# Two blocks of layers in fp32 on one core: order of the head's loads and squares, form of the last norm, and which engine makes the gate weights' remainders

## Chip, cores, metric

The kernel runs on one NeuronCore of a Trainium2 chip. The metric is the device time of one launch in microseconds; the median of several runs is compared. Engines are called TensorE (PE), VectorE (DVE), ScalarE (ACT), GpSimd (POOL) and SyncE (SP, which here issues DMAs).

## What is computed

256 tokens of width 1024 go through a first block (three mixers whose gated outputs are summed, and a feed-forward with a squared ReLU) and a second one (a convolution and pooling mixer, then a gated linear recurrence), all in fp32. What the change touches:

```python
def first_block(x, ...):
    h = rms_norm(x, norm1_g[l])          # the head
    u = h @ w_in[l]
...
def odd_mixer(h, w_in, conv_w, conv_b, w_rg, b_rg, w_ig, b_ig, lam, w_out):
    p = jnp.einsum("btd,dn->btn", h, w_in)
    xr, gate = jnp.split(p, [W_LRU], axis=-1)
    xc = causal_depthwise_conv(xr, conv_w, conv_b)
...
    _, hs = lax.associative_scan(_lin_combine, (a, bterm), axis=1)
    y = hs.astype(h.dtype) * jax.nn.silu(gate)
    return jnp.einsum("btn,nd->btd", y, w_out)
...
    return rmsnorm(h, final_norm)        # the last norm, 8 chunks of 128 features
```

## The kernel before

Activations lie transposed, 128 features by 256 tokens to a chunk, in a large SBUF tensor `arena`. A projection ("job") makes one chunk of outputs out of blocks of 128x128 weights. Eight blocks are a unit of 512 KB; SyncE fetches units 0 to 285 in order into a ring of five (`ring`, `RING`), unit `u` when the job that used unit `u - 5` is done.

Each fp32 product is made of three matmuls of fp32r parts: high weights by high data, high by low, low by high (L1750 to L1752). For that ScalarE copies a unit to its high part (`wsplit`, L887, `ring_hi`, three slots), and then GpSimd or VectorE subtracts to get the remainder (`remainder`, L553, written to `ring_lo`). Which of the two does a unit is said by `on_gpsimd`, in part by the unit's turn `hi_turn`, which counts from 1. Activations are split in the same way: high part on ScalarE (L908 with a gain, L910 without), remainder on VectorE (L1111) or GpSimd (L561).

`schedule()` writes one list of steps, and each engine goes through the whole list in order and does its own part of each step, waiting on semaphores. So an instruction that waits holds up all that stands behind it on its engine. A unit's `wsplit` stands `AHEAD` = 2 units before its job; that of the first two stood before the step `("nsq", 0, 4)`.

The head: `spin` is idle work for TensorE, `fills` are zero fills on VectorE, `split`/`lo` of `h0u` make x times its gain in two parts (not yet divided by the norm; the first eight jobs are scaled afterwards by `scale`, L1118), `nsq` squares a chunk on VectorE (L1078), `nsum` sums it on TensorE (L1504), `norm` is the root on ScalarE (L767) and the reciprocal on VectorE (L1094). `halves` are seven small scalings of parameters (L1081 to L1090). Then follow the token projections `tok` (L1515), the key norms `qsq`/`qap` (L1542, L1203), the compression inputs `cmp_in` (L1190) and matmuls `cmp_mm` (L1533), among the first `dq` jobs.

Near the end are twelve `xr` jobs (units 250 to 261), twelve `gate` jobs (262 to 273) and eight `odd_out` jobs of twelve blocks (274 to 285). In the xr loop VectorE does the convolution `oconv` (L1324 to L1330), the norm's `hf` (L1102) and `lw` (L1431, L1432); ScalarE the four functions of `rgi` (L949 to L955). In the gate loop VectorE does, for each job, `scan` (product L1443 of two SBUF chunks, scan L1444), `scanout` of two jobs before (L1437) and `gact` (L1455); ScalarE a tanh (L1009) and the split of `ly`, three jobs behind; GpSimd the remainder of that split (L561). Nine roots (`uroot`, L930) stand before gate job 0 and three behind job 5, each with a change of the function table. `rinv` (SBUF) and `rin` (PSUM) hold the reciprocal norm.

The last norm: after `odd_out` VectorE writes the reciprocal to PSUM and makes eight outputs with `hf` (L1102: chunk times gain times `rin`), stored two at a time.

## Time and profile before

| | us |
|---|---|
| median of 3 runs (1119.0 to 1123.94) | 1119.44 |
| the profiled execution | 1117.76 |
| its span, first to last instruction | 1116.0 |
| TensorE busy in the span | 1061.0 |
| VectorE busy | 725.9 |
| GpSimd busy | 603.5 |
| ScalarE busy | 591.6 |
| mean granted TensorE clock, of full speed | 0.981 |

Times in the trace are us from the span's start. A busy time includes time in which an instruction has started and is held by something outside its semaphores. "Idle before" is the time an engine stood still ahead of an instruction, with the instruction that ended it. TensorE's matmuls overlap, so their own lengths add up to more than their pace.

### The profile page before, as it was taken

To read this page: it belongs to the slowest core of one execution; us is meant where nothing else is said; L and a number is where in the kernel's file an instruction comes from. 1 tells how busy PE (TensorE), PEld (TensorE's weight loads), DVE (VectorE), ACT (ScalarE), POOL (GpSimd) and SP (SyncE) were. 2 spreads that over 40 slices of the span, in tenths; PEclk is the share of its full clock that TensorE was granted. 3 is DMA by queue.
4 is the path that set the end of the run, shared out by engine and by line. 5 is a ranking of instruction groups with operands and counts; after the bars stand their busy time and mean duration, and the time that the engine had idled before them with its cause. 6 is when DMAs were issued, how large, how long until landed. Compare 5 with 4: busy or idle time off the path is not lost. (4 is left out here: it accounts for less than half of the span.)

```text
span 1116.0 us, 21390 instructions
## 1 busy us (share of the span) xinstructions
PE 1061.0 (95%) x8189; PEld 996.0 (89%) x8189; DVE 725.9 (65%) x1494; ACT 591.6 (53%) x1178; POOL 603.5 (54%) x457
## 2 busy tenths in 40 slices
PE   8999999999999999989999999999998788999996
PEld 8799888888889998979999999999988787999986
DVE  7749587666653325784575553334999878678964
ACT  5335566766665467753445554335333436468741
POOL 3536444454445469544533444338677665467951
PEclk9989999999999999999999999999999989899999
DMA  8324332333233443235555555555444434544442
GB/s 302 99 89 139 126 115 95 114 115 114 97 113 127 139 133 100 91 99 173 183 161 181 187 183 177 182 178 170 157 164 154 130 113 132 176 146 146 156 136 74
DMA packets 43157, 158.08 MB, mean 142 GB/s; under 512 B 4912, under 2 KB 4912, under 8 KB 42672
## 3 DMA queue, kind: packets, MB, share of 16 engines
q1 hardware_dynamic: 42912, 156.69, 42.5%
q8 instruction: 65, 1.06, 0.4%
q14 instruction: 36, 0.29, 0.1%
q10 hardware_dynamic: 144, 0.03, 0.0%
HBM read 155.65 MB, written 1.05 MB: 140 GB/s over the span
## 5 line engine op out<-in xcount | busy, mean ns | idle before, releaser
L1750 PE MATMUL p_proj<-arena_r,ring_hi 128*128 128x256 f32 x2208 | 660.0, 299 | 19.9 <-POOL ring_lo L553 8.2
L1751 PE MATMUL p_proj<-arena_r,ring_hi 128*128 128x256 f32 x2208 | 627.7, 284 | 0.0
L1752 PE MATMUL p_proj<-arena_r,ring_lo 128*128 128x256 f32 x2208 | 627.6, 284 | 0.0
L553 POOL TENSOR_TENSOR ring_lo<-ring,ring_hi 128x1024 fp32r<-128x1024 f32 x182 | 437.0, 2402 | 308.0 <-ACT ring_hi L887 307.0
L1750 PEld LDWEIGHTS p_proj<-arena_r,ring_hi 128*128 128x128 f32 x2208 | 426.1, 193 | 39.3 <-issue 23.1
L1751 PEld LDWEIGHTS p_proj<-arena_r,ring_hi 128*128 128x128 f32 x2208 | 426.6, 193 | 8.1 <-issue 6.0
L1752 PEld LDWEIGHTS p_proj<-arena_r,ring_lo 128*128 128x128 f32 x2208 | 426.1, 193 | 0.0
L887 ACT ACTIVATE ring_hi<-ring 128x1024 fp32r<-128x1024 f32 x276 | 290.5, 1053 | 116.1 <-PE p_proj L1752 114.6
L553 DVE TENSOR_TENSOR ring_lo<-ring,ring_hi 128x1024 fp32r<-128x1024 f32 x94 | 118.4, 1260 | 70.7 <-ACT ring_hi L887 69.3
L661 POOL TENSOR_TENSOR sbuf_s<-sbuf_s,srow 128x256 f32<-128x256 f32 (+1 forms) x48 | 42.8, 892 | 83.5 <-DVE srow L1312 58.9
L910 ACT ACTIVATE arena_r<-arena 128x256 fp32r<-128x256 f32 x108 | 42.7, 409 | 44.8 <-DVE arena L1477 22.3
L561 POOL TENSOR_TENSOR arena_r<-arena,arena_r 128x256 fp32r<-128x256 f32 x64 | 51.5, 814 | 21.5 <-ACT arena_r L910 21.5
L908 ACT ACTIVATE arena_r<-arena,par 128x256 fp32r<-128x256 f32 x48 | 23.8, 505 | 63.4 <-DVE arena L1484 47.5
L1484 DVE TENSOR_TENSOR arena<-arena,p_proj 128x256 f32<-128x256 f32 x40 | 16.8, 421 | 62.3 <-PE p_proj L1752 61.6
L1300 DVE CUSTOM_DVE_ANT_0 sbuf_s<-p_score,caus,nrq 128x128 f32<-128x128 f32 (+1 forms) x64 | 24.2, 415 | 41.3 <-PE p_score L1595 39.3
L1399 DVE SCALAR_TENSOR_TENSOR p_score<-arena,par,p_score 128x256 f32<-128x256 f32 x116 | 46.9, 482 | 1.4
L1009 ACT ACTIVATE th<-p_proj 128x256 f32<-128x256 f32 x44 | 16.8, 383 | 54.4 <-PE p_proj L1752 54.4
L833 ACT ACTIVATE sbuf_s<-sbuf_s,srow 128x128 f32<-128x128 f32 (+1 forms) x96 | 42.6, 450 | 3.1 <-DVE srow L1300 3.1
L1737 PE MATMUL p_proj<-arena,ring 128*128 128x256 f32 x160 | 38.0, 390 | 5.7 <-issue 5.7
L1737 PEld LDWEIGHTS p_proj<-arena,ring 128*128 128x128 f32 x160 | 30.2, 195 | 10.4 <-issue 6.5
L1125 DVE SCALAR_TENSOR_TENSOR arena<-p_proj,rinv 128x256 f32<-128x256 f32 x32 | 13.6, 424 | 37.2 <-PE p_proj L1752 37.2
L561 DVE TENSOR_TENSOR arena_r<-arena,arena_r 128x256 fp32r<-128x256 f32 x44 | 27.1, 616 | 15.2 <-ACT arena_r L910 13.8
(272 smaller groups left out, 1218.4 us busy)
## 6 DMA issues: line engine op xcount, KB each, us to landing
ring<-w_stream SPq DMA_DIRECT2D x286, 512.0 KB, 3.3
arena<-w_tok SPq DMA_DIRECT2D x1, 1632.0 KB, 13.0
arena<-w_rgi SPq DMA_DIRECT2D x1, 1536.0 KB, 6.6
arena<-x_t SPq DMA_DIRECT2D x4, 256.0 KB, 4.8
arena<-w_cmp SPq DMA_DIRECT2D x1, 1024.0 KB, 16.3
out_t<-arena SPq DMA_DIRECT2D x4, 256.0 KB, 2.4
par<-cols SPq DMA_DIRECT2D x1, 323.0 KB, 3.3
row<-rows ACTq DMA_DIRECT2D x1, 32.0 KB, 3.5
```

The costliest lines, as they stand in the source:

```text
L553: return eng.tensor_tensor(ring_lo[:, u % RING, :, :].rearrange("p k n -> p (k n)"), ring[:, u % RING, :, :].rearrange("p k n -> p (k n)") ...
L561: return eng.tensor_tensor(lo(c), src(c), hi(c).bitcast(F32), ALU.subtract)
L661: pool.tensor_tensor(p, p, r.unsqueeze(2).to_broadcast([P, 2, kl]), ALU.mult)\
L833: ins = act.activation(p, p, ACT.Exp, bias=srow[:, i % 4, 2 + h:3 + h], scale=-1.0, accum_out=srow[:, i % 4, 4 + h:5 + h])
L887: act.activation(ring_hi[:, hi_slot[u], :, :].rearrange("p k n -> p (k n)"), ring[:, u % RING, :, :].rearrange("p k n -> p (k n)"), ACT.Copy)\
L910: ins = act.activation(hi(c), src(c), ACT.Copy)
L1300: ins = dve.tensor_tensor_reduce(out=x[:, h, :], in0=ps[:, h, :], in1=mask[:, t, 0:kl], scale=nrq[:, n:n + 1], scalar=-MARK, op0=ALU.add, ...
L1399: ins = dve.scalar_tensor_tensor(out=A(AC + cc) if tap == CONV_K - 1 else acc, in0=ub[:, cc, tap:tap + S], scalar=col("even_cw", CONV_K * ...
L1737: mm = pe.matmul(slot(s)[:, 0:S], ring[:, u % RING, b % 8, :], rhs[c], start=(c == 0), stop=(c == n - 1))
L1750: pe.matmul(slot(s)[:, 0:S], w_hi, hi, start=(c == 0), stop=False)
L1751: pe.matmul(slot(s)[:, 0:S], w_hi, lo, start=False, stop=False)
L1752: mm = pe.matmul(slot(s)[:, 0:S], w_lo, hi, start=False, stop=(c == n - 1))
```

## The change

Five things. In the head, SyncE fetches weight unit 0 before x and units 1 on behind it; the steps `wsplit` of units 0 and 1 get places of their own (`("units", 0)` before the splits of x, `("units", 1)` behind them), all eight squares stand behind both, all eight sums behind the first job, and the idle work of TensorE is 20 in one place instead of 12 and 10. `halves` moves from behind the eighth scaling to the seventh job (`n == 6`). The remainders of the first eight units, which went to VectorE at odd turns and to GpSimd at even ones, are swapped. The remainders of the gate units, all on GpSimd, go by turn; unit 262 has turn 253, so units 262, 264, ... 272 are VectorE's and 263, ... 273 GpSimd's. In the last norm ScalarE multiplies each chunk by its gain (`xg`, behind its root), and VectorE multiplies two chunks at once by the reciprocal norm (`hfin`); the stores wait for those. The last norm's reciprocal is written to PSUM as before.

```diff
--- before.py
+++ after.py
@@ -68,7 +68,7 @@
 ADDED_BY = {"h1": "w_out", "h2u": "ff2", "h3u": "even_ya"}
 
 
-HF_ROUND = {0: 0, 2: 1, 3: 2, 4: 3}
+HF_ROUND = {0: 0, 2: 1, 3: 2}
 
 
 PLAIN = {"b_val", "pool"}
@@ -106,26 +106,25 @@
         if tag:
             out.append(("lo", tag, 7))
 
-    out += [("spin", 12), ("fills", 0)]
+    out += [("spin", 20), ("fills", 0), ("units", 0)]
     for c in range(8):
-        if c < 4:
-            out += [("nsq", 0, c), ("split", "h0u", c), ("nsum", 0, c), ("lo", "h0u", c)]
-        else:
-            out += [("split", "h0u", c), ("lo", "h0u", c)]
-    out += [("spin", 10)] + [("nsq", 0, c) for c in range(4, 8)]
+        out += [("split", "h0u", c), ("lo", "h0u", c)]
+    out += [("units", 1)] + [("nsq", 0, c) for c in range(8)]
     for n, job in enumerate(HEAD):
         out.append(job)
         if n == 0:
-            out += [("nsum", 0, c) for c in range(4, 8)] + [("norm", 0)]
+            out += [("nsum", 0, c) for c in range(8)] + [("norm", 0)]
         else:
             out.append(("scale", HEAD[n - 1]))
         if 1 <= n <= 4:
             out += [("hf", 0, 2 * n - 2), ("hf", 0, 2 * n - 1)]
         if n == 4:
             out += [("fills", 1)]
+        if n == 6:
+            out.append(("halves",))
         if n >= 4:
             out += [("split", "h0", 2 * n - 8), ("split", "h0", 2 * n - 7)]
-    out += [("scale", HEAD[7]), ("halves",)]
+    out += [("scale", HEAD[7])]
     out += [("ksq", 0), ("ksq", 1), ("cmp_in", 0), ("tok", 0), ("qsq", 0), ("cmp_in", 1), ("qap", 0), ("ksq", 2),
             ("tok", 1), ("qsq", 1), ("cmp_in", 2), ("cmp_in", 3), ("qap", 1)]
     keys = {0: [("cmp_mm",)], 1: [("qsq", 2)], 2: [("qap", 2), ("ksq", 3)], 3: [("qsq", 3)], 4: [("softplus",)],
@@ -283,7 +282,7 @@
             out.append(("split", "ly", j - 3))
     out += [("scanout", 10), ("scanout", 11)] + [("split", "ly", c) for c in range(9, 12)]
     squared(4, jobs["odd_out"])
-    out += [("nsum", 4, 7), ("norm", 4)] + [("hf", 4, c) for c in range(8)] + [("store",)]
+    out += [("nsum", 4, 7), ("norm", 4)] + [("xg", c) for c in range(8)] + [("hfin", c) for c in range(0, 8, 2)]
 
     at, splits = 0, {}
     order = [s for s in out if s[0] == "job"]
@@ -293,7 +292,7 @@
     units = len(starts) // 8
     for u in range(units):
         if starts[8 * u][1] not in PLAIN:
-            splits.setdefault(("nsq", 0, 4) if u < AHEAD else starts[8 * (u - AHEAD)], []).append(("wsplit", u))
+            splits.setdefault(("units", u) if u < AHEAD else starts[8 * (u - AHEAD)], []).append(("wsplit", u))
     final = []
     for s in out:
         final += splits.get(s, []) + [s]
@@ -536,8 +535,10 @@
                 unit_of.setdefault(b // 8, s[1])
 
         def on_gpsimd(u):
-            if unit_of[u] in ("br_dsa", "dq", "nq", "val_glu", "b_gate", "a_gate", "even_yb", "xr", "gate"):
+            if unit_of[u] in ("br_dsa", "dq", "nq", "val_glu", "b_gate", "a_gate", "even_yb", "xr"):
                 return True
+            if unit_of[u] in ("iq", "ik", "dk", "kc", "vc", "ks", "kw"):
+                return hi_turn[u] % 2 == 1
             if unit_of[u] in ("xbc",):
                 return hi_turn[u] % 3 > 0
             return hi_turn[u] % 2 == 0
@@ -583,9 +584,10 @@
         @block.sync
         def _(sp_eng):
             sp_eng.dma_start(par[:, :], cols).then_inc(sem("par_in"), 16)
-            for c in range(0, 8, 2):
-                sp_eng.dma_start(arena[:, XT + c:XT + c + 2, :], x_t[:, c:c + 2, :]).then_inc(sem(f"x_in{c}"), 16)
             for u in range(n_units):
+                if u == 1:
+                    for c in range(0, 8, 2):
+                        sp_eng.dma_start(arena[:, XT + c:XT + c + 2, :], x_t[:, c:c + 2, :]).then_inc(sem(f"x_in{c}"), 16)
                 if u == RING:
                     sp_eng.dma_start(wtok, w_tok).then_inc(sem("wtok_in"), 16)
                     sp_eng.dma_start(wcmp, w_cmp).then_inc(sem("wcmp_in"), 16)
@@ -597,7 +599,7 @@
                 sp_eng.dma_start(ring[:, u % RING, :, :].rearrange("p k n -> p (k n)"),
                                  w_stream[u]).then_inc(w_in[u % RING], 16)
             for c in range(0, 8, 2):
-                sp_eng.wait_ge(sem("hf_ready"), 8 * HF_ROUND[4] + c + 2)
+                sp_eng.wait_ge(sem("out_ready"), c // 2 + 1)
                 sp_eng.dma_start(out[:, c:c + 2, :], arena[:, HF + c:HF + c + 2, :]).then_inc(sem("stored"), 16)
             sp_eng.wait_ge(sem("stored"), 64)
 
@@ -942,6 +944,11 @@
                     if j >= 4:
                         act.wait_ge(sem("lo_ff"), j - 3)
                     act.activation(A(FFS + j % 4), A(FFR + j % 4), ACT.Square).then_inc(sem("ffs_ready"), 1); note(sem("ffs_ready"))
+                elif k == "xg":
+                    c = s[1]
+                    was_read(act, ("job", "odd_out", c), "D")
+                    act.activation(A(HH + c), A(XT + c), ACT.Identity, scale=col("final_g", c))\
+                        .then_inc(sem("xg_ready"), 1); note(sem("xg_ready"))
                 elif k == "rgi":
                     h = s[1]
                     ps = take(s)
@@ -1068,7 +1075,7 @@
             ths = [0]
             for s in steps:
                 k = s[0]
-                if k not in ("nsq", "lo", "hf"):
+                if k not in ("nsq", "lo", "hf", "hfin"):
                     settle()
                 if k == "nsq":
                     _, q, c = s
@@ -1094,14 +1101,19 @@
                     link(dve.reciprocal(rin if s[1] == 4 else rinv[:, :], root[:, 0, :]))
                 elif k == "hf":
                     _, q, c = s
-                    if c == 0 and q < 4:
+                    if c == 0:
                         link(dve.tensor_scalar(rin, rinv[:, :], 1.0, None, ALU.mult))
                     if q == 0:
                         dve.wait_ge(sem("par_in"), 16)
-                    g = {0: "norm1", 2: "even_g", 3: "odd_g", 4: "final_g"}[q]
+                    g = {0: "norm1", 2: "even_g", 3: "odd_g"}[q]
                     dve.scalar_tensor_tensor(out=A((HF0 if q == 0 else HF) + c), in0=A(XT + c), scalar=col(g, c),
                                              in1=rin, op0=ALU.mult, op1=ALU.mult)\
                         .then_inc(sem("hf_ready"), 1); note(sem("hf_ready"))
+                elif k == "hfin":
+                    c = s[1]
+                    dve.wait_ge(sem("xg_ready"), c + 2)
+                    dve.tensor_tensor(A(HF + c, 2), A(HH + c, 2), rin.unsqueeze(1).to_broadcast([P, 2, S]), ALU.mult)\
+                        .then_inc(sem("out_ready"), 1); note(sem("out_ready"))
                 elif k == "lo":
                     _, tag, c = s
                     src, hi, lo, _, _ = parts[tag]
```

## Rows read from the trace of the kernel before

**Rows 1.** The page, its first part: busy us, share of the span, instructions.
```profile
PE 1061.0 (95%) x8189; PEld 996.0 (89%) x8189; DVE 725.9 (65%) x1494; ACT 591.6 (53%) x1178; POOL 603.5 (54%) x457
```

**Rows 2.** Stretches: busy us (count) of PE, PEld, DVE, ACT, POOL; PEclk; DMA share; GB/s.
```profile
20.00:38.20 18.20, 18.20 (x153) 18.20 (x152) 11.05 (x23) 11.82 (x24) 11.62 (x8) 1.00 0.60 201
38.20:56.46 18.26, 14.93 (x61) 9.41 (x60) 17.41 (x31) 3.88 (x8) 7.74 (x7) 1.00 0.16 55
56.46:63.40 6.94, 6.94 (x65) 6.88 (x65) 3.56 (x5) 0.00 (x0) 0.00 (x0) 0.50 0.04 15
...
63.60:66.60 3.00, 3.00 (x15) 3.00 (x16) 0.00 (x0) 1.40 (x4) 1.50 (x1) 0.50 0.00 0
...
1041.00:1064.00 23.00, 22.12 (x173) 20.86 (x171) 21.97 (x30) 16.48 (x28) 21.87 (x15) 1.00 0.49 166
```

**Rows 3.** Time line of the head: start us, length us, engine, line, operation.
```profile
8.41 2.57 DVE L1111 SCALAR_TENSOR_TENSOR arena_r<-arena,par,arena_r 128x256 fp32r<-128x256 f32 x5
...
9.15 0.91 ACT L908 ACTIVATE arena_r<-arena,par 128x256 fp32r<-128x256 f32 x2 [0.97 <-DMA arena<-x_t]
...
10.66 1.06 ACT L887 ACTIVATE ring_hi<-ring 128x1024 fp32r<-128x1024 f32 x1 [0.60 <-DMA ring<-w_stream]
...
13.06 2.40 POOL L553 TENSOR_TENSOR ring_lo<-ring,ring_hi 128x1024 fp32r<-128x1024 f32 x1 [6.91 <-ACT ring_hi L887]
...
13.08 3.67 DVE L1078 TENSOR_TENSOR arena<-arena 128x256 f32<-128x256 f32 x4
...
13.20 1.06 ACT L887 ACTIVATE ring_hi<-ring 128x1024 fp32r<-128x1024 f32 x1 [0.22 <-DMA ring<-w_stream]
...
17.67 0.47 PE L1750 MATMUL p_proj<-arena_r,ring_hi 128*128 128x256 f32 x1
```

**Rows 4.** Time line behind the head; in brackets the idle time before and its releaser.
```profile
38.28 0.43 DVE L1118 TENSOR_TENSOR p_proj<-p_proj,rinv 128x256 f32<-128x256 f32 x1 [2.45 <-PE p_proj L1752]
...
44.56 0.70 PE L1542 MATMUL p_pv<-th,mean_h 128*128 128x256 f32 x2 [0.91 <-DVE th L1198]
...
56.46 6.99 PE L1533 MATMUL p_score<-arena 128*64 128x30 f32 x64 [2.42 <-DVE arena L1190]
```

**Rows 5.** L1443 alone (DVE busy, PEclk, DMA, GB/s); L1443, L561: ns min/median/max.
```profile
1020.00:1070.00 50.00, 15.32 (x12) 1.00 0.48 158
...
L1443 DVE TENSOR_TENSOR p_turn<-arena x4: 432/1566/2482, 1028.0 to 1059.5; 128x256 f32<-128x256 f32 x4
...
L561 POOL TENSOR_TENSOR arena_r<-arena,arena_r x64: 713/740/1777, 31.0 to 1070.7; 128x256 fp32r<-128x256 f32 x64
```

**Rows 6.** Time lines of ScalarE, GpSimd and VectorE from the xr projections on.
```profile
1018.39 0.43 DVE L1324 TENSOR_TENSOR p_proj<-p_proj,rinv 128x256 f32<-128x256 f32 x1
...
1019.53 1.05 ACT L887 ACTIVATE ring_hi<-ring 128x1024 fp32r<-128x1024 f32 x1
...
1031.71 0.43 DVE L1431 SCALAR_TENSOR_TENSOR p_score<-p_score,arena 128x256 f32<-128x256 f32 x1 [2.52 <-ACT arena L955]
...
1045.40 2.40 POOL L553 TENSOR_TENSOR ring_lo<-ring,ring_hi 128x1024 fp32r<-128x1024 f32 x1
...
1048.64 2.40 POOL L553 TENSOR_TENSOR ring_lo<-ring,ring_hi 128x1024 fp32r<-128x1024 f32 x1
...
1062.74 1.23 DVE L553 TENSOR_TENSOR ring_lo<-ring,ring_hi 128x1024 fp32r<-128x1024 f32 x1
...
1069.06 0.88 DVE L1437 SCALAR_TENSOR_TENSOR arena<-p_pv,arena 128x256 f32<-128x256 f32 x2
```

**Rows 7.** Time line of the last norm, and the group of L1345.
```profile
1108.16 1.76 DVE L1094 RECIPROCAL p_mean<-root 128x256 f32<-128x256 f32 x1 [1.37 <-ACT root L767]
...
1109.96 3.22 DVE L1102 SCALAR_TENSOR_TENSOR arena<-arena,par,p_mean 128x256 f32<-128x256 f32 x8
...
L1345 DVE TENSOR_TENSOR arena<-p_turn,sp 128x512 f32<-128x512 f32 x8 | 5.5, 691 | 4.1 <-PE p_turn L1634 3.9
```

## Prediction

> **What bounds the kernel now.** I read the page first, then the busy time in stretches, then the time lines of the four engines side by side where the diff touches them, at both ends and in the gate projections. TensorE is busy 95% of the span [rows 1], so the static list of matmuls sets the time, and a change can only pay in the places where TensorE waits or runs at its lower clock. The stretches show which places near the diff are like that [rows 2]: from 38.20 to 56.46 TensorE has 14.93 of 18.26 us busy while VectorE has 17.41; from 56.46 to 63.40 it is busy but at half the clock; from 1041 to 1064 VectorE has 21.97 of 23.00 us and GpSimd 21.87, with TensorE at 22.12. Everywhere else near the edits the four engines have room.
>
> One mechanism decides all parts. A subtraction of a whole weight unit costs 2.40 us on GpSimd and 1.23 us on VectorE [rows 3, 6], but a VectorE instruction with both inputs in SBUF stands still while GpSimd works, and the other way round. The squares at 13.08 are four instructions of some 0.43 us and take 3.67 us, because GpSimd holds from 13.06 to 15.46 [rows 3]. In the gates the product L1443 takes 1566 ns in the median of its form and 432 ns undisturbed [rows 5]. The instructions with an operand in PSUM (L1437, L1455) show no such stretch. At 1062.74 VectorE's subtraction starts and GpSimd's part, ready at the same time, waits for it.
>
> **The head: first weights ahead of x.** Before, the last of x has landed at 9.15 and unit 0 at 10.66, as the starts of ScalarE's copies show [rows 3]. The bytes up to the last of x and unit 0 are the same, so I let x's last piece land at about 10.4 and unit 0 at about 5.5. GpSimd (unit 0 now has its turn) subtracts from 6.65 to 9.05; this holds back VectorE's eight remainders of x, which have both inputs in SBUF. They cost 2.57/5 = 0.51 us each [rows 3], so they run from 9.05 to 13.1, and the first projection, chunk by chunk behind them, ends at about 13.5 instead of 16.1. The rest gives that back. VectorE does unit 1 next (13.1 to 14.35). ScalarE's copy of unit 2 ends at 14.26 as before [rows 3], GpSimd waits with unit 2 and takes the port until 16.75, and only then come the squares, now eight instead of four: 16.75 + 8 x 0.43 = 20.2. All eight sums stand in TensorE's list ahead of the second projection, which so starts at about 20.55 instead of 17.67: **+2.9**. In this gap TensorE has one sum to do in about 3.5 us. The clock fell at 56.46 after an idle time of 2.42 us [rows 2, 4], so I expect it to fall here too. A projection matmul takes 3.00/15 = 0.20 us then against 18.20/153 = 0.12 us [rows 2]; some 3.4 us at the low level cost about **+1.5** (0 if it does not fall, +3.0 if it stays down twice as long).
>
> The seven projections after that are one unbroken row (17.67 to 38.2) and only shift. Behind them VectorE is late: after 38.28 it does the halvings, with TensorE idle 0.91 at 44.56 and 2.42 at 56.46 [rows 4]. The halvings move ahead of that, into VectorE's idle time (2.45 us of it stand before 38.28, and more behind the earlier projections). Then VectorE is no longer late and both stalls go: **-3.3** (between -2.0, if another subtraction lands on L1190, and -3.3). Without the 2.42 us of idle time the compression matmuls (L1533, 64 of them in 6.99 us at the low clock) start at the high one. No row shows them there: at best 3.5 us are saved and 1.5 more on the projection behind them, at least nothing. Their 30 columns are few, and they kept the clock down for 7 us, so I take half of 5.0: **-2.5**. Head: +2.9 + 1.5 - 3.3 - 2.5 = **-1.4**, between -5.4 (2.9 - 3.3 - 5.0) and +3.9 (2.9 + 3.0 - 2.0). The second batch of VectorE's zero fills and the longer spin cost nothing: both lie in time in which their engine has no data yet.
>
> **The gates.** Before, all twelve remainders are GpSimd's. One round is 1048.64 - 1045.40 = 3.24 us on GpSimd, against 24 x 0.12 = 2.88 on TensorE, and VectorE, whose own share is 3.24 - 1.14 = 2.10, waits 1.57 - 0.43 = 1.14 us for the port in its product [rows 5, 6]. VectorE also ends the stage: its last two scan outputs end at 1069.94 [rows 6], and TensorE waits for what follows from them. So I count VectorE's chain. It gets six subtractions of 1.26 with their gaps: +7.6. Unit 262 comes first, where the convolution of 1018.39 stands now, but ScalarE's copy of it runs from 1019.53 to 1020.58 [rows 6]: +2.3 of waiting. Unit 264 must wait until the copies behind the nine roots are done, and takes up the 2.52 us that VectorE idles before 1031.71: -2.5. The port waits of before, 15.32 - 12 x 0.43 = 10.2 us in twelve products [rows 5], go: -10.2. New ones come. In a pair of rounds VectorE has 2 x 2.10 + 1.26 = 5.46 us to do with its two products 1.6 to 1.7 us from the next port user on either side, and GpSimd's 2.40 us fit in no such hole. I walked the four queues from 1018.39 to the end with these durations, letting whoever waits take the port first. It gave ten port waits of 0.2 to 0.9 us, 4.8 to 6.2 us together by how the durations are rounded. With 5.3 the last scan output ends at about 1072.4, **+2.5**: 7.6 + 2.3 - 2.5 - 10.2 + 5.3. In this walk two subtractions (units 268 and 272) meet GpSimd's part within 0.05 us. If GpSimd is first, its own subtraction then slips in behind, and VectorE's next product waits 2.4 us: +1.75 each. At 1062.74 VectorE was first by 0.04 us. I add half a case: **+3.4**, between -2.5 (TensorE's pace in all seven saturated rounds, 7 x 0.36) and +6.0 (both).
>
> The Trainium skill, SBUF — State Buffer, "Who interferes with whom", calls this a lock which whoever starts first holds for its whole instruction, with the other fully blocked. By that rule alone two rounds hold the port 2 x (2.40 + 0.74 + 0.35) = 7.0 us before and 2.40 + 1.23 + 2 x 1.09 = 5.8 us after, so an estimate from port time alone would be a gain of 3 to 4 us; the trace's two rounds of 6.48 us are shorter than the rule's 7.0, so a part of the small instructions overlaps. What speaks against that gain is VectorE's order, which the rule leaves out. The same skill, Perfetto Trace Analysis, "Optimizing Scalar/DVE Operations", warns that moving work between these two engines might not help, since they share a read port.
>
> **The last norm.** Before, the reciprocal ends at 1109.92 and eight products take 3.22 us to 1113.18 [rows 7]. After, four products of two chunks: the nearest row is L1345, 691 ns for 128x512 with one operand in PSUM; 4 x 0.69 + 3 x 0.03 = 2.85. ScalarE's eight gains stand behind its root (which ends 0.1 us before 1108.16) in its queue; at 0.45 us each [rows 3] the last ends at 1111.65, and the fourth product, due at 1112.05, is not held. The store follows the last product as before: **-0.4** (0 to -0.8).
>
> **Sum.** -1.4 + 3.4 - 0.4 = +1.6 us. The profiled execution took 1117.76 us for its span of 1116.0, and the median of the runs is 1119.44, so it is 1.7 below it; I add the sum to the median: **1121.0 us**.
>
> **Rivals.**
> - *The gates pay.* TensorE gets its 2.88 us rounds, since GpSimd has 2.40 + 2 x 0.74 = 3.9 us [rows 5] in 5.76, and VectorE's waits vanish: -2.5 for the saturated rounds, and up to -1.2 in the first four. With the best head (-5.4) this is -8 to -9, **1111**. For it: GpSimd goes from one subtraction to the next without a gap. Against: VectorE has no gap there either, and its own 5.46 us leave 0.3 us in 5.76.
> - *The remainders are trapped* (the other side: slower). Each VectorE subtraction waits for GpSimd's part and then lets GpSimd's 2.40 us in ahead of the next product. It decides when GpSimd is first at units 268 and 272: gates +6.0; with a clock that stays down for two stretches in the head and no gain at the compression, +3.9 there: **1129** at worst, 1124 with the middle head.
> - *The head only loses.* The start is late by 4.4 to 5.9 and only the stalls of 3.3 come back: +1.1 to +2.6 instead of -1.4, total **1123.5 to 1125**. It decides if the compression runs at 1.2 GHz as before.
> - *Nothing is seen.* Both ends move inside the waits and the gates keep 3.24 us: **1119**.
>
> **How the numbers follow.** The forecast (parts nearly cancel, 1118 to 1123) has 0.50; the gates pay 0.14; trapped 0.12; the head only loses 0.14; nothing is seen 0.10. The bound of 0.5%, about what a measurement of this kernel tells from no change, is 5.6 us. Only the far ends of the first two rivals pass it, and an unknown clock fall adds to both: faster 0.12, same 0.76, slower 0.12. The range takes the forecast, the head's loss and the near halves of the two others: 1114.5 to 1126.
>
> **What would show it.** Right: the second projection starts at 20 to 22 us; VectorE's squares stand in one block after GpSimd's unit 2; TensorE has no idle time at L1542 and L1533; six L553 on VectorE between 1018 and 1064, one with over 2 us of waiting for ScalarE; the last L1437 later than 1069.9 relative to the tenth xr projection; four hfin products of 0.69 us. Wrong: the squares end by 18 us (then the head gains 2 to 3 us more); gate projections 2.88 us apart with VectorE idle between products; a clock that stays low for some 10 us in either place, which I could not bound from the rows.

## The result, and the profile after

| | before | after |
|---|---|---|
| median of 20 runs each, us | 1118.26 | 1122.61 |
| lowest and highest | 1115.78 to 1123.94 | 1119.9 to 1126.01 |
| the profiled execution, its span | 1117.76, 1116.0 | 1121.83, 1120.1 |
| mean granted TensorE clock | 0.981 | 0.977 |

The ratio is 1.0039 with a 95% interval of 1.003 to 1.0049: the change costs about 4.4 us, between 3.4 and 5.5. That lies inside the 5.6 us that I had called no change. The forecast was 1121.0, with a sum of +1.6 us. Line numbers move by 1 to 12: L553 is L554 now, L887 L889, L1078 L1085, the halvings (L1081 to L1090) L1088 to L1097, L1094 L1101, L1190 L1202, L1437 L1449, L1443 L1455, L1504 L1516, L1533 L1545, L1750 L1762; the last products are L1115.

The busy time in stretches after the change (us, busy time and instructions of five engines, granted clock, DMA share, GB/s); the third to fifth answer to [rows 2]:

```profile
16.60:19.00 2.40, 2.39 (x9) 2.05 (x10) 2.30 (x7) 0.00 (x0) 0.00 (x0) 0.80 0.99 418
19.00:21.70 2.70, 2.70 (x10) 2.14 (x8) 0.00 (x0) 0.00 (x0) 0.00 (x0) 0.55 0.82 331
42.60:60.40 17.80, 14.86 (x62) 9.65 (x61) 17.10 (x29) 4.69 (x11) 7.98 (x7) 1.00 0.18 61
60.40:65.80 5.40, 5.39 (x65) 5.34 (x65) 3.57 (x5) 0.00 (x0) 0.00 (x0) 0.69 0.01 3
1043.50:1066.50 23.00, 22.60 (x177) 21.38 (x176) 21.84 (x35) 16.15 (x28) 17.22 (x12) 1.00 0.54 176
1073.00:1080.00 7.00, 6.87 (x32) 6.67 (x33) 4.32 (x5) 3.55 (x5) 4.04 (x4) 0.53 0.11 28
```

The gap that the halvings were to close is still open (TensorE 14.86 of 17.80 us), the compression has a mean clock of 0.69, and the gates run a little fuller (22.60 of 23.00 us against 22.12). The time lines of the head, to be set beside [rows 3] and [rows 4]; the last line is the same place in the time line of TensorE:

```profile
13.98 4.92 DVE L1085 TENSOR_TENSOR arena<-arena 128x256 f32<-128x256 f32 x8
13.94 2.34 POOL L554 TENSOR_TENSOR ring_lo<-ring,ring_hi 128x1024 fp32r<-128x1024 f32 x1 [5.18 <-ACT ring_hi L889]
16.61 5.41 PE L1516 MATMUL p_mean<-arena,mean_d 128*128 128x256 f32 x16 [3.26 <-DVE arena L1085]
21.67 0.47 PE L1762 MATMUL p_proj<-arena_r,ring_hi 128*128 128x256 f32 x1
60.41 5.36 PE L1545 MATMUL p_score<-arena 128*64 128x30 f32 x64 [2.95 <-DVE arena L1202]
```

GpSimd's unit 2 starts 0.04 us ahead of the squares and the first sum can begin only at 16.61, behind it. From there it is not the squares that count, as I had thought: they end at 18.90, while the eight sums (two records each) take 5.41 us, part of them at the low clock, and the second projection starts at 21.67, 4.00 us later than before. The row of projections behind it is not unbroken either: TensorE waits 0.37 us at 36.78 for a remainder from GpSimd.

What VectorE then does ahead of the token projections:

```profile
37.75 0.90 DVE L1130 TENSOR_TENSOR p_proj<-p_proj,rinv 128x256 f32<-128x256 f32 x2
38.68 0.37 DVE L1088 TENSOR_SCALAR half<-par 128x16 f32<-128x16 f32 x1
...
40.52 2.31 DVE L1092 TENSOR_SCALAR par<-par 128x24 f32<-128x24 f32 x1
42.86 0.64 DVE L1094 TENSOR_TENSOR half<-par 128x8 f32<-128x8 f32 x1
...
44.21 2.28 DVE L1097 TENSOR_SCALAR half<-par 128x3 f32<-128x3 f32 x1
46.52 0.90 DVE L1130 TENSOR_TENSOR p_proj<-p_proj,rinv 128x256 f32<-128x256 f32 x2
```

The seven halvings run from 38.68 to 46.49 without a pause and hold up the last two scalings until 46.52. The last projection of the head is over at 42.6, so VectorE is late much as before (4.8 us, against 5.8 from 38.28 to 44.08). Then the gates, and TensorE's waits in and behind them:

```profile
1023.20 1.23 DVE L554 TENSOR_TENSOR ring_lo<-ring,ring_hi 128x1024 fp32r<-128x1024 f32 x1 [2.33 <-ACT ring_hi L889]
1027.08 0.38 PE L1762 MATMUL p_proj<-arena_r,ring_hi 128*128 128x256 f32 x1 [1.60 <-DVE arena L1342]
1035.38 0.38 PE L1762 MATMUL p_proj<-arena_r,ring_hi 128*128 128x256 f32 x1 [0.56 <-DVE arena L1342]
1053.28 1.23 DVE L554 TENSOR_TENSOR ring_lo<-ring,ring_hi 128x1024 fp32r<-128x1024 f32 x1
1054.54 0.85 DVE L1455 TENSOR_TENSOR p_score<-arena 128x256 f32<-128x256 f32 x1
1059.66 1.22 DVE L554 TENSOR_TENSOR ring_lo<-ring,ring_hi 128x1024 fp32r<-128x1024 f32 x1
1072.31 0.88 DVE L1449 SCALAR_TENSOR_TENSOR arena<-p_pv,arena 128x256 f32<-128x256 f32 x2
1114.37 2.48 DVE L1115 TENSOR_TENSOR arena<-arena,p_mean 128x512 f32<-128x512 f32 x4
```

VectorE waits 2.33 us for the copy of unit 262, as forecast, and the convolutions behind it are late, so TensorE waits 1.60 and 0.56 us for their results (L1342); before, it waited 0.42 us in this stretch. A pair of rounds is 1059.66 - 1053.28 = 6.38 us against 6.48. The four last products take 2.48 us instead of 3.22.

**Where the time went.** Every weight unit has one copy on ScalarE (L889 after, L887 before). How much later it starts than the copy of the same unit in the first trace of before gives a course through the execution. Columns are times of the trace before; "gates" is the difference between 1019.5 and 1062.6.

| later than before by, us | 36.2 | 69.7 | 496 | 834 | 1019.5 | 1062.6 | 1096 | end of span |
|---|---|---|---|---|---|---|---|---|
| after | 4.77 | 2.40 | 2.39 | 0.65 | 2.51 | 3.24 | 4.41 | 4.06 |
| E1 head alone | 5.11 | 2.75 | 2.80 | 1.05 | 2.52 | 2.54 | 2.52 | 2.52 |
| E2 gates alone | -0.40 | -0.21 | -0.17 | -0.88 | 3.74 | 4.47 | 4.45 | 4.47 |
| E3 norm alone | -0.31 | -0.11 | -0.08 | -0.80 | 1.10 | 1.12 | 1.16 | 0.80 |
| E4 halvings at the seventh job | -0.67 | -2.48 | -2.45 | -2.44 | 0.42 | 0.44 | 0.50 | 0.51 |
| E5 sums late | 2.63 | 1.76 | 1.81 | 0.08 | 1.69 | 2.42 | 3.57 | 3.21 |
| E6 idle work in the gap | 3.37 | 2.52 | 2.56 | 1.91 | 3.23 | 3.97 | 5.12 | 4.76 |
| E7 halvings at the start | 5.62 | 1.63 | 1.66 | -0.06 | 1.85 | 2.58 | 3.77 | 3.40 |
| E8 two units back | -0.16 | 0.05 | 0.08 | 0.11 | 0.26 | 2.77 | 3.19 | 3.22 |
| E9 halvings early, norm | 1.14 | -2.50 | -4.52 | -3.04 | -1.83 | -1.78 | -1.86 | -2.22 |
| E10 other turn | -0.42 | -1.74 | -1.71 | -2.35 | 1.61 | 3.16 | 2.22 | 2.24 |
| E11 before, again | -0.42 | -0.39 | -2.37 | -2.36 | -0.69 | -0.60 | -0.63 | -0.62 |

The last row is the scale for all others: the same kernel, profiled twice, moves against itself by up to 2 us in places that no edit touches. The difference over the gates alone repeats much better: they cost 0.73 or 0.74 us in all five kernels that have the changed turns (after, E2, E5, E6, E7), and at most 0.09 where they are untouched. The column 69.7 does not repeat so well: with the head of before it stands between -0.39 and 0.05 in E2, E3, E8 and E11, and at -1.74 in E10, whose clock stayed low for a shorter time at the compression.

### The profile page after: what moved, and what is told of

It is laid out like the page before. It is cut to its first block and busy times, and to the rows that moved or that the text cites. A ratio compares the mean times of both kernels' runs of the same rounds, so it can differ in the third digit from the quotient of the medians.

```text
span 1120.1 us, 21393 instructions
## 1 busy us (share of the span) xinstructions
PE 1063.5 (95%) x8185; PEld 998.3 (89%) x8185; DVE 733.2 (65%) x1496; ACT 594.6 (53%) x1186; POOL 593.8 (53%) x451
## 3 DMA queue, kind: packets, MB, share of 16 engines
HBM read 155.65 MB, written 1.05 MB: 140 GB/s over the span
## 5 line engine op out<-in xcount | busy, mean ns | idle before, releaser
L1762 PE MATMUL p_proj<-arena_r,ring_hi 128*128 128x256 f32 x2208 | 662.2, 300 | 18.7 <-POOL ring_lo L554 7.6
L554 POOL TENSOR_TENSOR ring_lo<-ring,ring_hi 128x1024 fp32r<-128x1024 f32 x176 | 424.4, 2413 | 318.6 <-ACT ring_hi L889 317.8
L1762 PEld LDWEIGHTS p_proj<-arena_r,ring_hi 128*128 128x128 f32 x2208 | 427.6, 194 | 38.1 <-issue 19.8
L889 ACT ACTIVATE ring_hi<-ring 128x1024 fp32r<-128x1024 f32 x276 | 290.5, 1053 | 117.2 <-PE p_proj L1764 114.1
L554 DVE TENSOR_TENSOR ring_lo<-ring,ring_hi 128x1024 fp32r<-128x1024 f32 x100 | 124.5, 1245 | 71.6 <-ACT ring_hi L889 70.0
L562 POOL TENSOR_TENSOR arena_r<-arena,arena_r 128x256 fp32r<-128x256 f32 x64 | 54.1, 855 | 24.9 <-ACT arena_r L912 24.8
L912 ACT ACTIVATE arena_r<-arena 128x256 fp32r<-128x256 f32 x108 | 42.6, 408 | 45.5 <-DVE arena L1489 22.5
L835 ACT ACTIVATE sbuf_s<-sbuf_s,srow 128x128 f32<-128x128 f32 (+1 forms) x96 | 42.6, 450 | 3.1 <-DVE srow L1312 3.1
```

What stands on the lines that cost most here:

```text
L554: return eng.tensor_tensor(ring_lo[:, u % RING, :, :].rearrange("p k n -> p (k n)"), ring[:, u % RING, :, :].rearrange("p k n -> p (k n)") ...
L562: return eng.tensor_tensor(lo(c), src(c), hi(c).bitcast(F32), ALU.subtract)
L835: ins = act.activation(p, p, ACT.Exp, bias=srow[:, i % 4, 2 + h:3 + h], scale=-1.0, accum_out=srow[:, i % 4, 4 + h:5 + h])
L889: act.activation(ring_hi[:, hi_slot[u], :, :].rearrange("p k n -> p (k n)"), ring[:, u % RING, :, :].rearrange("p k n -> p (k n)"), ACT.Copy)\
L912: ins = act.activation(hi(c), src(c), ACT.Copy)
L1762: pe.matmul(slot(s)[:, 0:S], w_hi, hi, start=(c == 0), stop=False)
```

## The experiments

Times are medians; ratios are against runs of before on the same chip, with 95% intervals. They are not the quotients of the medians, from which they differ by up to 0.001 (E4). E1 to E4 and E8 to E10 are built on the kernel before, E5 to E7 on the changed one.

**E1, the head part alone** (every hunk of the diff on the head, loads and turns of the first eight units; nothing else).

> The kernel before with the whole head part alone (loads, squares and sums behind job 0, halves at the seventh job, swapped turns). Theory A (the loss of the change lies mostly in the head): the trace of the changed kernel shows TensorE 2.4 us later behind the compression matmuls and the offset is 2.5 us before the gates, so this kernel is +2.5 us against before (ratio 1.0022), between +2 and +3.5. Theory B (the head is neutral and the loss comes from the gates and clock falls far behind it): within 1 us of before.

1122.48 against 1118.69 us, ratio 1.0042 (1.0025 to 1.0059). The trace is 2.75 us late behind the compression and 2.5 at the end; the time says 2.8 to 6.6 us. The head loses, and theory B falls. No run takes the head's own parts (loads, swapped turns, squares) one by one; E5 to E7 move the sums, the idle work and the halvings.

**E2, the gate turns alone.**

```diff
-            if unit_of[u] in (..., "even_yb", "xr", "gate"):
+            if unit_of[u] in (..., "even_yb", "xr"):
                 return True
```

> The kernel before with the gate remainders by turn, nothing else. Theory A (VectorE's chain is a little longer, as the changed kernel's last scan output 0.74 us later relative to its offset, and a second stretch at the low clock behind it): +0.7 us from VectorE and up to +1.2 from the clock, so +0.7 to +2.0 us. Theory B (the longer low clock behind the gates in the changed kernel has nothing to do with the turns): +0.7 us and a low stretch of one piece as before. Rival (gates pay): -2.5 or better.

1120.63 us, ratio 1.0014 (1.0000 to 1.0029). In the trace the stage costs 0.73 us; the low clock behind it is one short piece as before, so the longer one after the change (0.53 over 7 us, above) is not the turns' alone. The other 2.8 us of this trace come between 972 and 997 us, where nothing was changed: its clock falls at 986, and E10, the only other trace with that fall, loses the same there. The gates do not pay.

**E3, the last norm alone** (the hunks with `xg`, `hfin`, `out_ready`).

> The kernel before with the last norm's new form alone. Theory A: four products of 0.60 to 0.62 us instead of eight of 0.40, -0.7 us. Theory B: the gains on ScalarE delay the products or the stores land later, so nothing of it reaches the end: 0 +- 0.3 us.

1117.9 us, ratio 0.9998 (0.9986 to 1.0009). The time cannot tell; the trace can: from 1096 us to the end it gains 0.36 us (1.16 to 0.80), and after, E5, E6, E7 and E9, which have this norm too, gain 0.35 to 0.38. Theory A has the products right (-0.74) and forgets that half of it is lost behind them: from the last product to the end of the span it takes 3.25 us after the change, against 2.86 before.

**E4, only the place of the halvings.**

```diff
+        if n == 6:
+            out.append(("halves",))
...
-    out += [("scale", HEAD[7]), ("halves",)]
+    out += [("scale", HEAD[7])]
```

> The kernel before with the step halves moved to the seventh job, nothing else. My prediction's step: the halvings fall into VectorE's idle time before 38.28, both TensorE stalls of 0.91 and 2.42 us go and the compression matmuls start at the high clock: -3.3 to -6 us. Rival (what the changed kernel's trace hints at: the halvings run in port waits beside GpSimd's subtractions and push VectorE's scalings behind them): one stall goes, the other stays, -2 to 0 us.

1118.29 us, ratio 1.0006 (0.9992 to 1.0019). VectorE's time line, and TensorE's at the compression:

```profile
33.25 0.89 DVE L1083 TENSOR_SCALAR half<-par 128x16 f32<-128x16 f32 x1
...
35.60 2.29 DVE L1087 TENSOR_SCALAR par<-par 128x24 f32<-128x24 f32 x1
...
39.27 2.28 DVE L1092 TENSOR_SCALAR half<-par 128x3 f32<-128x3 f32 x1
41.59 0.90 DVE L1120 TENSOR_TENSOR p_proj<-p_proj,rinv 128x256 f32<-128x256 f32 x2
55.51 5.73 PE L1535 MATMUL p_score<-arena 128*64 128x30 f32 x64 [2.85 <-DVE arena L1192]
```

In the kernel before the halvings stand behind the scaling of 38.28 [rows 4] and last from 38.75 to 44.05. One of them is held there too (time line of VectorE, kernel before):

```profile
39.97 2.31 DVE L1083 TENSOR_SCALAR half<-par 128x96 f32<-128x96 f32 x1
```

Moved, they last 8.3 us instead of 5.3, since GpSimd's subtractions of a unit hold them twice and those of activations slow the rest. The rival is right about the stalls: that of 0.91 is gone, that of 2.42 is 2.85. From the second projection to the compression this trace takes 38.05 us; five traces with the head of before (E2, E3, E8, E10, E11) take 38.54 to 38.58. So the edit gains 0.5 us there, and the rest of the -2.48 in the table is an earlier start and, as in E10, a shorter low clock at the compression.

**E5, sums behind the second projection.**

```diff
-        if n == 0:
-            out += [("nsum", 0, c) for c in range(8)] + [("norm", 0)]
-        else:
-            out.append(("scale", HEAD[n - 1]))
+        if n == 1:
+            out += [("nsum", 0, c) for c in range(8)] + [("norm", 0), ("scale", HEAD[0])]
+        if n >= 1 and n != 1:
+            out.append(("scale", HEAD[n - 1]))
```

> The changed kernel, with the eight sums, the root and the first scaling behind the second projection instead of the first. Theory A (the head loses because all eight sums stand in TensorE's list ahead of the second projection, and the gap ahead of them has nothing to do): the second projection starts at 14.0 instead of 21.67, the sums (8 x 0.47) run behind it from about 17.0 to 20.8, the third projection starts at about 20.8 instead of 24.7, the clock does not fall at 18.3, so 3.5 to 4 us are gained at the eighth projection and about 3.5 at the end: ratio to before about 1.0005. Theory B (the first scaling and root, now later, hold up the later scalings and VectorE's backlog grows): the stall ahead of the compression matmuls grows by what the head gained, and the end comes 0 to 1 us earlier.

1120.97 us, ratio 1.0024 (1.0013 to 1.0035). TensorE:

```profile
14.55 0.38 PE L1762 MATMUL p_proj<-arena_r,ring_hi 128*128 128x256 f32 x1 [0.64 <-DVE ring_lo L554]
17.51 3.61 PE L1516 MATMUL p_mean<-arena,mean_d 128*128 128x256 f32 x16
24.43 0.38 PE L1762 MATMUL p_proj<-arena_r,ring_hi 128*128 128x256 f32 x1 [0.44 <-ACT arena L977]
27.95 0.35 PE L1762 MATMUL p_proj<-arena_r,ring_hi 128*128 128x256 f32 x1 [0.39 <-POOL ring_lo L554]
34.64 0.35 PE L1762 MATMUL p_proj<-arena_r,ring_hi 128*128 128x256 f32 x1 [0.53 <-POOL ring_lo L554]
```

The second projection starts at 14.55, the clock does not fall there, and the third projection starts at 20.78, against 24.73 after the change, as theory A says. But then weights and scalings are late three times, 1.36 us together, and 2.1 of the 3.9 us gained are left at 36 us. They are still there when the compression starts (58.28 against 60.41), behind a stall of 2.96 us that has not grown against 2.95. So theory A has the cause, the sums were in the way; theory B is right that later waits take a part, and wrong about the stall. The next 1.5 us go inside the compression, whose matmuls take 7.00 us here against 5.36 (see E6).

**E6, idle work in the gap.**

```diff
-            out += [("nsum", 0, c) for c in range(8)] + [("norm", 0)]
+            out += [("spin", 13)] + [("nsum", 0, c) for c in range(8)] + [("norm", 0)]
```

> The changed kernel with 13 idle matmuls of 128 columns (0.24 us each, 3.1 us) in TensorE's gap between the first projection and the first sum. Theory A (TensorE's gap of 3.26 us brings the clock down at 18.33, and the sums, not the squares, set the start): no low clock there, the eight sums take 8 x 0.47 = 3.8 us from 16.6, the second projection starts at 20.4 instead of 21.67, -1.3 us. Theory B (the clock falls for another reason, or the idle matmuls push the sums): the second projection starts at 21.5 or later.

1121.7 us, ratio 1.0028 (1.0015 to 1.0040). TensorE:

```profile
13.60 3.06 PE L1508 MATMUL p_pv<-mean_d,ones 128*128 128x128 f32 x26
16.89 3.72 PE L1516 MATMUL p_mean<-arena,mean_d 128*128 128x256 f32 x16 [0.23 <-DVE arena L1085]
```

Eight sums in 3.72 us at full clock instead of 5.41: theory A. The head's last projections start 1.4 us earlier than after the change (3.37 against 4.77), and the compression too (59.01 against 60.41), behind the same stall (2.94 against 2.95). At 69.7 none of it is left (2.52 against 2.40). It goes inside the compression, where the clock is low for longer. Ten us from its first matmul on, in this trace and, second line, in the one after the change (granted clock last but two):

```profile
59.00:69.00 10.00, 9.99 (x81) 9.94 (x82) 3.57 (x5) 1.51 (x4) 1.89 (x1) 0.53 0.01 2
60.40:70.40 10.00, 9.99 (x91) 9.94 (x91) 3.57 (x5) 1.51 (x4) 2.37 (x1) 0.66 0.01 2
```

The three traces in which the clock falls in the sums (after, E1, E7) have the shorter low stretch at the compression, E5 and E6 the longer one. The head of before shows both, without a fall in the sums (0.51 over ten us in E11, 0.66 in E10), so whether E6's loss belongs to its edit or to chance is open.

**E7, halvings at the start.**

```diff
-    out += [("spin", 20), ("fills", 0), ("units", 0)]
+    out += [("spin", 20), ("fills", 0), ("units", 0), ("halves",)]
...
-        if n == 6:
-            out.append(("halves",))
```

> The changed kernel with the seven halvings right behind the first zero fills (5.3 us) instead of at the seventh job. Theory A (at the seventh job they take 7.8 us because GpSimd's subtractions hold them twice for 2.3 us and they push two scalings behind them; ahead of x VectorE idles 2.7 us with GpSimd free): the halvings take at most 3 us, the seventh and eighth scalings end 7 us earlier, the 2.95 us of idle time before the compression matmuls goes, -2.9 us at that place. Theory B (they run beside GpSimd's first subtraction from 6.4 and hold up the remainders of x): the first projection starts 1 to 3 us later and at most 1 us is left.

1120.65 us, ratio 1.0019 (1.0009 to 1.0029). VectorE, and TensorE at the compression:

```profile
6.22 0.18 DVE L1087 TENSOR_SCALAR half<-par 128x24 f32<-128x24 f32 x1
6.43 0.21 DVE L1088 TENSOR_SCALAR half<-par 128x96 f32<-128x96 f32 x1
6.67 2.23 DVE L1090 TENSOR_SCALAR par<-par 128x24 f32<-128x24 f32 x1
...
45.53 5.62 DVE L1200 TENSOR_TENSOR arena<-arena,par 64x120 f32<-64x120 f32 x8
59.65 5.22 PE L1543 MATMUL p_score<-arena 128*64 128x30 f32 x64 [1.33 <-DVE arena L1200]
```

Between the two theories. One halving is caught by GpSimd's unit 0, and the head is 0.85 us later. The stall ahead of the compression falls from 2.95 to 1.33, not to 0: with the halvings gone, the compression inputs meet GpSimd's subtractions and take 5.62 instead of 3.28 us. Net -0.8 us at 69.7.

**E8, units 262 and 264 left on GpSimd.**

```diff
-            return hi_turn[u] % 2 == 0
+            return hi_turn[u] % 2 == 0 or u in (262, 264)
```

> The kernel before with the gate remainders by turn, but units 262 and 264 left on GpSimd. By my sum the two cost VectorE 2 x 1.26 + 2.3 of waiting - 2.5 of idle time used = 2.3 us. Theory A (VectorE's chain sets the end of the gates): the last scan output comes 1 to 2.3 us earlier than with all six, so about 1 us before that of the kernel before, and the time is -0.5 to -1.5 us. Theory B (TensorE's or GpSimd's chain took over, as the four rounds with 262 to 265 on GpSimd are 3.24 us each): the last scan output stays where six put it, +0.7.

1121.37 us, ratio 1.0029 (1.0017 to 1.0041). The interval overlaps that of all six (E2, 1.0000 to 1.0029); in the trace the stage costs 2.51 us against 0.73, against both theories. VectorE and, last, GpSimd:

```profile
1037.97 1.23 DVE L553 TENSOR_TENSOR ring_lo<-ring,ring_hi 128x1024 fp32r<-128x1024 f32 x1
1039.23 2.57 DVE L1443 TENSOR_TENSOR p_pv<-arena 128x256 f32<-128x256 f32 x1
1039.12 2.39 POOL L553 TENSOR_TENSOR ring_lo<-ring,ring_hi 128x1024 fp32r<-128x1024 f32 x1 [3.58 <-ACT ring_hi L887]
```

This is the trap of my second rival: VectorE subtracts unit 266, GpSimd's unit 267 gets in ahead of the next product, and that stands still until 1041.51. In the kernel before GpSimd begins unit 266 at 1035.87, 1.8 us ahead of VectorE here (1037.97, less the 0.27 by which this trace is late).

**E9, halvings where GpSimd is idle, and the new norm; no other part of the change.**

```diff
+        if n == 2:
+            out.append(("halves",))
         if 1 <= n <= 4:
...
-    out += [("scale", HEAD[7]), ("halves",)]
+    out += [("scale", HEAD[7])]
```

> The kernel before with the halvings behind the scaling of the third job (about 24.0, where GpSimd has nothing to do until 25.95 and VectorE idles 2.46 us later on) and the new last norm; loads, squares and gates as before. Theory A (the halvings' price is the port: undisturbed they take 0.17 to 0.8 us each): they take at most 2.5 us, nothing behind them moves, both stalls go (0.91 and most of 2.42 us), -3 us ahead of the compression matmuls, -1 to -2 in the end stretch of them, -0.7 for the norm: the time is -2 to -4 us against before. Theory B (time gained in the head is given back by the clock farther on, as the profile of the kernel with the halvings moved alone hints, 2.5 us ahead at 850 us and 0.4 behind at 970): the trace is 3 us ahead until 840 us, and the time is within 0.1% of before.

1116.7 us, ratio 0.9983 (0.9972 to 0.9994): some 1.9 us faster than before (0.7 to 3.1), and below the interval of the changed kernel. VectorE, and TensorE's two remaining waits:

```profile
23.97 0.17 DVE L1088 TENSOR_SCALAR half<-par 128x16 f32<-128x16 f32 x1
...
25.25 0.23 DVE L1097 TENSOR_SCALAR half<-par 128x3 f32<-128x3 f32 x1
36.04 0.35 PE L1762 MATMUL p_proj<-arena_r,ring_hi 128*128 128x256 f32 x1 [0.84 <-POOL ring_lo L555]
55.53 5.01 PE L1545 MATMUL p_score<-arena 128*64 128x30 f32 x64 [1.69 <-DVE arena L1202]
```

The seven halvings take 1.51 us from 23.97 on. What was left out of theory A is again what they displace: ScalarE's next instruction waits for the scaling behind them, a unit is 0.84 us late, and the stall at the compression is 1.69 instead of 2.42. The instructions behind the old place now meet GpSimd instead, as the compression inputs show, which took 2.93 us before:

```profile
41.51 5.62 DVE L1202 TENSOR_TENSOR arena<-arena,par 64x120 f32<-64x120 f32 x8
```

So from the second projection to the compression this trace takes 37.94 us, 0.6 less than those five traces and only 0.1 less than E4, though the halvings cost 1.5 us here and 8.3 there. Of the 2.5 us at 69.7 the rest is not the edit's: E10, with the head of before and as short a low clock, has -1.74. The trace explains about 1.0 us (0.6 and the norm's 0.36), which the timed interval holds. No run has the early halvings without the norm.

**E10, the other turn in the gates.**

```diff
+            if unit_of[u] == "gate":
+                return hi_turn[u] % 2 == 1
             return hi_turn[u] % 2 == 0
```

> The kernel before with the gate remainders by turn, but VectorE has units 263, 265, ... 273 and GpSimd 262, 264, ... 272. Theory A (VectorE's sum of work decides: 7.6 us of subtractions without the 2.3 us of waiting for ScalarE's copy of unit 262): the last scan output comes 1 to 2.3 us earlier than with the even turns, time -1.5 to 0 us against before. Theory B (what decides is which of two subtractions that become ready together is first and who is trapped behind it, as where 266 went to VectorE at 1037.97 and GpSimd's 267 came at 1039.12 ahead of the next product): at least one product of 2.4 us or more stands behind a VectorE subtraction before 1045, and the gates cost +1 to +3 us.

1119.82 us, ratio 1.0013 (1.0000 to 1.0026). The stage costs 1.55 us in the trace, against 0.73 with the even turns and 2.51 in E8. Theory A falls: as many subtractions on VectorE and less waiting (1.52 us for ScalarE's copy instead of 2.33), and yet 0.8 us later at the end of the stage. By time E10 and E2 cannot be told apart (1.0013 and 1.0014); in this trace the clock also stays up from 1069 to 1078 us (1.00 against 0.81 before), which takes 0.9 us back. Theory B has the size, not the picture: the longest product is 1.63 us, and TensorE's waits are spread (0.53, 1.02, 0.38 and 0.68 us, all for remainders).

**E11, the kernel before once more.**

> The kernel before, a second profile. Theory A (the falls of the clock of 3.4 us that differ from trace to trace, as at 494, 842 and 986 us, come by chance and each costs about 1.5 us): this trace has the same times as the first up to the first such difference, and other falls somewhere in it. Theory B (they belong to the kernel's order): the same falls at the same places, 125, 872, 906, 947 and 1070 us.

1117.17 us. The granted clock (last but two) in the first trace of before and, second fence, in this one:

```profile
490.00:494.00 4.00, 2.34 (x15) 1.74 (x14) 3.72 (x11) 1.81 (x5) 0.00 (x0) 1.00 0.38 126
840.00:844.00 4.00, 1.00 (x9) 0.90 (x8) 3.90 (x10) 1.33 (x2) 3.92 (x3) 1.00 0.40 134
870.00:878.00 8.00, 6.16 (x31) 5.54 (x32) 6.57 (x17) 2.08 (x3) 1.37 (x2) 0.79 0.21 67
```

```profile
490.00:494.00 4.00, 3.99 (x29) 3.46 (x28) 3.77 (x6) 3.97 (x8) 1.64 (x1) 1.00 0.37 131
840.00:844.00 4.00, 3.20 (x15) 3.23 (x16) 3.90 (x11) 0.00 (x0) 4.00 (x3) 0.61 0.09 36
870.00:878.00 8.00, 7.00 (x38) 6.45 (x39) 5.74 (x15) 2.57 (x5) 2.21 (x1) 0.79 0.19 66
```

Neither theory is whole. The falls at 125, 872, 906, 947 and 1070 us are in both traces. That at 840 is in the second only, and by ScalarE's copies it goes with a loss of 1.5 us between 834 and 864. Of the thirteen traces it is in all but the first and E8's; the one at 1070 is missing in E10. Near 494 us the first trace lost 2 us without any fall. So a single trace of before is no zero line to better than 2 us.

## Why the prediction was right, and where it was not

The total was right within its range, 1122.61 against 1121.0 (1114.5 to 1126), and so was "same" by the bound of 0.5%. The sum behind it was less good: +1.6 us against 4.4. Part of the close total is luck: I added the sum to the median of three runs, 1119.44, and twenty runs of before give 1118.26. Step by step:

- **Start of the second projection, +2.9 and +1.5 for the clock.** Measured +4.0 (21.67 against 17.67), where the sum had 20.55 and the rest of the clock's cost behind it; at 36.2 the trace is 4.8 late. The size is right, the place is not: I let the squares set the start and counted the sums at nothing but the last. Eight sums take 3.72 us at full clock (E6) and 5.41 with the fall; four of them stood in TensorE's idle time before. The clock costs 1.7 us in the sums (5.41 against 3.72), and without its fall the second projection starts 1.4 earlier (20.26, E6). The wait of 0.37 us for GpSimd at 36.78, where I had said that the projections only shift, makes most of the rest of the 4.8.
- **The halvings, -3.3.** This is the step that failed. I had the idle time of VectorE at that place and not GpSimd's: the halvings take 5.3 us in before, 7.8 after and 8.3 in E4, but 1.51 where GpSimd is idle (E9). That one of them was already held for 2.31 us at 39.97 in the kernel before (E4) was there to be seen. So only the stall of 0.91 went, and that of 2.42 became 2.95. The mechanism was the one that I had put ahead of all parts and used for the squares and the gates; I did not apply it to a step that moved. Nor would their price have been the whole answer: where it is put right (E9) the stall of 1.69 stays, since the compression inputs meet GpSimd then, and the gain is 0.6 us instead of 3.3, against 0.5 in E4.
- **The compression at the high clock, -2.5.** This credit was misplaced. The matmuls took 5.36 instead of 6.99 us, -1.6, but not because the stall was gone: it was longer. Traces with the head of before and the same stall of 2.42 or 2.43 us show 6.99, 7.00 (E11), 6.76 (E8), 5.98 (E2), 5.92 (E3) and 5.05 us (E10), and those with the changed head 5.36, 5.63 (E1), 7.00 (E5), 6.45 (E6) and 5.22 (E7). Where in the work the clock falls differs from execution to execution of the same head, so the 1.6 us cannot be booked as an effect of the change; that 1.6 of the 2.5 came is luck.
- **Head.** Forecast -1.4; the trace has +2.4, E1 by time 1.0025 to 1.0059, 2.8 to 6.6 us. That is the size of my rival "the head only loses" (1123.5 to 1125, chance 0.14), but not its reason: it let both stalls go and the compression stay low, and what happened is that the longer stall stayed. In this trace the head is +4.0 at the second projection, +4.0 when the compression starts and +2.4 behind it.
- **Gates, +3.4.** Measured +0.73 five times. The wait of 2.33 us, the six subtractions and their places came as forecast; the port waits that I put at 5.3 us were smaller: in each of the four pairs of rounds after 1047 two products take 0.85 and 0.87 instead of 0.43 us, about 3.4 us together, and those ahead of 1047 hardly wait. With 3.4 for 5.3, and without the half case of a trapped remainder, my sum gives 7.6 + 2.3 - 2.5 - 10.2 + 3.4 = +0.6, which is what came. VectorE was first at each of its units and the trap never closed, while in E8 it did. The Trainium skill, SBUF — State Buffer, "Who interferes with whom", says that the engine that holds the shared ports blocks the other for its whole instruction, and the traces agree: a halving of 0.2 us stands 2.3 us beside a subtraction of 2.4. My estimate of 5.8 us for two rounds from port time alone does not hold: they take 6.38, and VectorE has no idle time in them, so its own list sets them. Against my own reason, though, the sum of VectorE's work does not rank the variants either: E10 has less waiting in it than E2 and E8 less work, and in the traces both leave the stage later (1.55 and 2.51 us against 0.73, one trace each).
- **A longer stretch at the low clock behind the gates,** 1.2 us between 1062.6 and 1096, was in no step. It is in after, E5, E6 and E7 and in neither E1 nor E2, so it needs both the later head and the turns, or it is a matter of when in the execution the stage comes; no run here separates these.
- **Last norm, -0.4.** Measured -0.35 to -0.38 in the six traces that have it; the products take 0.62 us, not 0.69, and the stores give half of it back.

The terms that the traces repeat add up to 2.4 to 2.75 for the head, 0.7 for the gates and -0.35 for the norm, about +2.8 to +3.1; the medians differ by 4.4 (3.4 to 5.5). The longer low clock would close most of the gap, but it is the one term that I could not pin to a part. Against the second trace of before, which has the fall at 840 as the changed kernel has, the same account closes: 2.8 behind the compression, 0.4 up to 1019.5, 0.6 in the gates, 1.2 at the longer low clock and -0.35 in the norm make 4.7 us of span. That is one trace against one, and shows how far the zero line matters.

## What to carry to other kernels

Idle time of an engine is only free for an instruction if its neighbour on the same port is idle too: look at both time lines before a filler is moved, and at what it displaces. The seven fillers cost 8.3 us beside GpSimd's subtractions (E4) and 1.5 beside an idle GpSimd (E9), yet the bottleneck, TensorE, reached the compression only 0.1 us sooner for it, because what stood behind them met the next subtractions. So count the wait of the bottleneck engine, not the price of the filler. E9, the early place with the new norm, is the only variant whose interval lies below the kernel before. When two queues are coupled like that, a sum of work doesn't rank schedules; run the two or three nearest variants. And profile the kernel before twice: a difference of 2 us in one trace, from the clock above all, need not be the kernel's.

## What the hardware showed that I had not expected

- Halvings of 1 to 96 columns take 0.16 to 0.23 us with GpSimd idle, 0.61 to 0.70 beside its subtractions of 128x256 and 2.2 to 2.3 beside one of 128x1024. The one of 1 column pays the same as that of 96. After the change the seven stand beside seven GpSimd instructions in a row, one each, so their number counts and not their size.
- Eight fp32 sums of 256 columns took 3.72 us at the full clock and 5.41 where the clock fell in their midst.
- The fall of the clock at the compression comes in every trace, with a stall of 1.33 to 2.96 us ahead of it, and the same 64 matmuls take 5.01 to 7.00 us by where it starts.
